# The start address of one operand: the token sums of the second feed-forward part, from 128 to 64 modulo 256 bytes

## The reference

```python
def _swiglu(x, w_gate, w_up, w_down):
    return (jax.nn.silu(x @ w_gate) * (x @ w_up)) @ w_down

h = _layer_norm(ALPHA * h + 0.5 * _swiglu(h, ffn2_w_gate[l], ffn2_w_up[l], ffn2_w_down[l]),
                ln4_g[l], ln4_b[l])
```

## Time and profile before

| | us |
|---|---|
| median of 3 runs | 1694.38 |
| lowest, highest run | 1690.96, 1695.35 |
| profiled execution | 1696.59 |
| its span, first to last instruction | 1694.9 |
| PE busy in the span | 1674.2 (99%) |
| DVE busy | 1098.7 (65%) |
| ACT busy | 742.0 (44%) |
| frames of the second feed-forward part | about 805 to 1002 us of the span |

### The profile page before, as it was taken

How to read it: one execution, slowest core, us unless ns; L and a number is a source line. 1 busy time by engine, 2 the same in 40 slices (tenths; PEclk the granted TensorE clock), 3 DMA queues, 4 the chain that set the end, 5 groups by cost and what they waited for, 6 DMA issues and landing times.

```text
span 1694.9 us, 24997 instructions
## 1 busy us (share of the span) xinstructions
PE 1674.2 (99%) x9222; PEld 1414.9 (83%) x9222; DVE 1098.7 (65%) x1489; ACT 742.0 (44%) x1099; POOL 167.8 (10%) x158
## 2 busy tenths in 40 slices
PE   9999999999999999998999999999999999999999
PEld 8888888788887888877999998877778787788887
DVE  5333338987974693669788774457976969744442
ACT  5222222246454374535555563345555455733231
POOL 0000000102005621013000001022101020000000
PEclk9999999999999999999999999999999999999999
DMA  6332347743121344232323335323232222233331
GB/s 217 99 99 89 96 136 227 221 136 107 63 90 60 125 149 137 90 97 67 108 99 114 109 113 164 108 88 119 84 100 84 87 90 80 79 121 112 107 105 63
DMA packets 51482, 188.13 MB, mean 111 GB/s; under 512 B 5776, under 2 KB 6288, under 8 KB 50512
## 3 DMA queue, kind: packets, MB, share of 16 engines
q1 hardware_dynamic: 44640, 161.50, 30.1%
q10 hardware_dynamic: 5184, 16.00, 3.0%
q0 software_dynamic: 1584, 9.60, 1.6%
HBM read 182.89 MB, written 4.19 MB: 110 GB/s over the span
## 4 chain that ended last, share of the span: by engine, by line
PE 51%; DVE 1%; issue 0%; ACT 0%
PE proj L439 41%; PE aux L439 6%; PE aux L2312 1%; PE aux L2299 1%; PE aux L2289 1%; PE aux L2292 0%; PE aux L583 0%; DVE xraw L1376 0%; DVE xsum L1381 0%; DVE hm L721 0%; PE aux L2337 0%; PE proj L2332 0%; PE aux L2327 0%; DVE a_lo L727 0%; DVE w_lo L431 0%
## 5 line engine op out<-in xcount | busy, mean ns | idle before, releaser
L431 DVE TENSOR_TENSOR w_lo<-raw,w_hi 128x1024 fp32r<-128x1024 f32 x260 | 331.3, 1276 | 305.4 <-ACT w_hi L424 299.8
L439 PE MATMUL proj<-a_hi,w_hi 128*128 128x512 f32 (+1 forms) x1336 | 510.4, 382 | 3.4 <-DVE a_lo L926 1.8
L439 PE MATMUL proj<-a_hi,w_lo 128*128 128x512 f32 (+1 forms) x1336 | 501.0, 375 | 0.0
L439 PE MATMUL proj<-a_lo,w_hi 128*128 128x512 f32 (+1 forms) x1336 | 500.6, 375 | 0.0
L424 ACT ACTIVATE w_hi<-raw 128x1024 fp32r<-128x1024 f32 x257 | 270.0, 1053 | 223.1 <-PE proj L439 146.4
L439 PEld LDWEIGHTS proj<-a_hi,w_hi 128*128 128x128 f32 x1336 | 251.6, 188 | 55.1 <-issue 5.5
L439 PEld LDWEIGHTS proj<-a_lo,w_hi 128*128 128x128 f32 x1336 | 251.3, 188 | 46.0 <-issue 2.9
L439 PEld LDWEIGHTS proj<-a_hi,w_lo 128*128 128x128 f32 x1336 | 251.0, 188 | 45.6
L439 PE MATMUL proj<-hid_hi,w_hi 128*128 128x512 f32 (+1 forms) x374 | 142.9, 382 | 1.4 <-DVE w_lo L431 1.4
L439 PE MATMUL proj<-hid_hi,w_lo 128*128 128x512 f32 (+1 forms) x374 | 141.0, 377 | 0.0
L439 PE MATMUL proj<-hid_lo,w_hi 128*128 128x512 f32 (+1 forms) x374 | 141.0, 377 | 0.0
(11 more groups left out here) (419 smaller groups left out, 2720.6 us busy)
## 6 DMA issues: line engine op xcount, KB each, us to landing
raw<-stream SPq DMA_DIRECT2D x303, 512.0 KB, 3.6
ctxk<-ada_in ACTq DMA_DIRECT2D x12, 512.0 KB, 4.3
ctxv<-ada_in ACTq DMA_DIRECT2D x12, 512.0 KB, 4.3
out<-h ACTq DMA_DIRECT2D x7, 256.0 KB, 2.0
h<-x_in SPq DMA_DIRECT2D x3, 512.0 KB, 8.6
btab<-rpb_in POOLq DMA_DIRECT2D x4, 384.0 KB, 3.5
cond_row<-cond_in ACTq DMA_DIRECT2D x1, 1024.0 KB, 6.2
side<-mem_in POOLq DMA_DIRECT2D x1, 1024.0 KB, 5.1
```

The costliest lines, as they stand in the source:

```text
L431: nc.vector.tensor_tensor(w_lo[:, st.slot], raw[:, st.slot], w_hi[:, st.slot].bitcast(F32), ALU.subtract).then_inc(lo_ready, 1)
L439: mm = nc.tensor.matmul(dst, a, b, start=start and n == 0, stop=stop and n == 2, skip_group_check=seeded)
```

## The change

One allocation of 48 float32 (192 bytes) per partition is put ahead of `xsum`. The `xsum` tensor starts at byte 193856 in place of 193664: at 64 modulo 256, as `ctx_hi` and `ctx_lo` do, in place of 128. Nothing is allocated after it in its phase, so no other tensor moves. The instructions of every engine, their order, their shapes and their waits are the same as before; the address of one operand differs in 960 matmuls, four ACT copies and four DVE subtractions.

```diff
             corner = sb("corner", [P, 2, HT], F32, ph)
             tsum = sb("tsum", [P, 3, T], F32, ph)
+            sb("under_xsum", [P, 48], F32, ph)
             xsum = sb("xsum", [P, 4, 2, 4, HT], F32R, ph)
```

## The result

| | before | changed |
|---|---|---|
| median, us | 1693.13 | 1696.03 |
| lowest, highest | 1688.76, 1697.4 | 1694.31, 1699.1 |
| runs | 22 | 22 |

The ratio is 1.0019, with a 95% interval of 1.0013 to 1.0026. I had forecast 1690.3 us, 4.1 us faster; it came out 2.9 us slower, by less than the 0.3% that I had set as the bound of "no change", but clear of noise over 22 runs. The spread says something too: the kernel before covers 8.6 us, the changed one 4.8.

A forecast was written before the change was run, and what follows sets the result against it. The prediction took PE's own matmul rate as the bound. Its terms, -4.3 us on the xsum matmuls and +0.16 us at the down projection, summed to -4.1 us: 1690.3 us from the median of 1694.4, range 1686.3 to 1695.8.

The forecast's parts named there:

- s = 113.3 ns: Frames, 960 matmuls moving xsum: step falls from 117.8 ns to the context rows' 113.3, saving 4.3 us.
- The 117.8 ns of the frames: Step per matmul in the frames before the change, read from two starts 16 frames apart, 158.30 us.
- its 2.2 us: Profiled execution's excess over the runs' median of 1694.4 us; the forecast was counted from the median.
- The rival of the distance: Frames: operand starts alike modulo 128 give xsum matmuls 120.0 ns, 2.1 us slower, 1696.5 us; chance 0.11.
- The 720 plain matmuls: Frames, matmuls moving the plain tokens: both addresses kept, so no change; neighbour effects costed at nothing.
- Who must keep up: Helpers in the frames: paced by PE; tightest handover, the corner sum, 1.64 us early, margin shrinking by 0.05 us.
- My own forecast frame: Changed kernel's frames: 16 should take 154.9 us in place of 158.3.
- the rival of the adding savings: Frames: savings of both starts add, xsum step 111.1 ns, 6.4 us saved less 0.24, 1688.2 us; chance 0.25.
- The writes of xsum: Eight instructions writing xsum before the frames: under 0.1 us by the destination's start, costed at nothing.
- The wait at the down projection: First matmul after the frames waits for DVE's weight split: 1.03 in place of 0.87 us, losing 0.16 us.
- 16-byte rule: SBUF has 16-byte cachelines and stepping between them costs; every start here is alike, so the change gives 0 us.
- independent read ports: Separate array ports for moving and stationary operands: stationary start should not matter, so 113.3 ns holds, 4.3 us saved.

The follow-up runs named there:

- after_again: The changed kernel, nothing edited, traced in a second execution: 1696.55 us.
- before_again: The kernel before the change, nothing edited, traced in a second execution: 1691.51 us.
- pairs: Computation left out: only 256-column matmuls, 96 for each of 16 pairs of moving and stationary starts, run twice in opposite orders; steps 113.3 to 120.0 ns.
- before_third: The kernel before the change, nothing edited, traced in a third execution: 1692.24 us.
- reset_x4: The kernel before with one of four sums, X4, moved 64 bytes further, its quarter at distance 0: median 1691.58 us, ratio 0.9985.

## Why the prediction was wrong

- *"I take s = 113.3 ns: it is the one row with this moving start, and the change is an alteration of the moving start."* This step failed. The rows held two addresses each, and I let one of them explain the difference. The quantity is their distance; the change took the sums from 64 to 128, where the step is 118.7 ns, and 118.8 was measured in the frames, in place of 113.3. The term was put at -4.3 us. Against the slow pattern that I had profiled it is 960 x (118.8 - 117.8) = +1.0 us, against the fast one 960 x 5.5 = +5.3.
- *The 117.8 ns of the frames* I took for the property of the kernel before. It was one of two patterns, and this execution stayed in it throughout. Two more showed 154.3 and 154.5 us for 16 frames, not 158.3. The sign that I passed over stood in the times: three runs spread over 4.4 us, and the profiled one was above all of them. I subtracted its 2.2 us as a constant; the slow pattern has a part in them, how large a part the timed runs don't show.
- *The rival of the distance* had the mechanism and the sign: +2.1 us forecast, +2.9 measured. I had given it 0.11. That the two numbers are near is luck: it counted from 117.8 ns, left the plain matmuls alone and had 120.0 ns for the sums (I reckoned modulo 128) against 118.7. I argued it down with "frames and context rows have the same distance, ... and yet 117.8 and 113.3 ns; so the distance can't be all". Equal distances with unequal steps should have led to the thought that the step has two values.
- *The 720 plain matmuls "keep both addresses: no change"*: wrong. They went from 117.8 to 115.5 ns on the mean, though their own distance stayed 64: the three plain quarters of a frame have 115.4, 117.8 and 113.3 ns, the same in every frame behind the first of both executions. What lies around them matters, and the quarter directly ahead is not all of it, since that is a sum quarter for each of the three. They gave back 720 x 2.3 = 1.7 us against the slow pattern, which is why the two profiled executions look alike: +1.0 - 1.7 us gives the 0.5 to 0.7 us that the frames gained there. Against the fast pattern they lost 720 x 2.2 = 1.6 us. My term was nothing, with a reason (six changes of kind in a frame) that took the effect to reach one matmul; it reaches whole quarters.
- *Who must keep up*: right for the changed kernel, whose 9.86 us frames the helpers keep up with, wrong as a statement on 113.3 ns frames. I let the margin shrink by 0.05 us once; it shrinks by the difference of two periods in every frame, 9.60 - 9.52 = 0.08 us, and with the 0.6 us that went at once in the fourth frame 1.25 us were gone in a dozen frames. My own forecast frame, 154.9 / 16 = 9.68 us, would have stayed above the helpers' 9.60; the rival of the adding savings, 153.2 / 16 = 9.58, would have met that bound.
- *The writes of xsum* cost nothing, as said. The wait at the down projection was 1.01 us in the first trace, near the 1.03 forecast, but 0.88 in after_again, hardly more than before's 0.87; since the sum quarters did not get faster, the 1.01 does not bear the forecast out.
- The Trainium skill's 16-byte rule (SBUF — State Buffer, "Door 1: The DMA port swizzle") gave 0 us. The runs do not agree with it as a rule for matmuls: starts that are all multiples of 16 give 113.3 to 120.0 ns. The Trainium skill's independent read ports (TensorE: Matmul & The Clock Gate, "Step-by-step: what each phase is for") are not borne out in the same table, where nothing but the place of one operand relative to the other moves the step by 6.7 ns.

How the 2.9 us come about is then, I take it, a mean over executions. In both traces of the changed kernel 16 frames take 157.76 us; in the three of before they take 154.3 to 158.3. Over all 20 frames the changed kernel (after_again) loses 3.8 us to before_again and gains 0.6 on the execution of the earlier trace rows (195.00 us). A median difference of 2.9 lies between the two. Which pattern each of the 22 timed runs was in was not traced. The pattern is also not all that spreads the runs: the lower clock at the head of the frames cost nothing in one trace, 1.3 us in another and 2.6 in the third, and ahead of it, at 788 us, the three traces of before already lie up to 1.8 us apart.

## What to carry to other kernels

A step read from one execution may be one of several that the same code can have: look first at how far the timed runs spread and where the profiled one lies among them, and profile a second and a third execution before a fraction of a per cent is argued. Of two operands' addresses ask for their distance before either start, and measure the pairs by themselves: one small kernel with all 16 pairs would have shown 118.7 ns where this forecast put 113.3. A gain in rate on the busiest engine ends where its helpers' own round begins, and a margin is used up by the difference of the two periods in every turn, not once.

## What the runs showed of the hardware that I had not expected

- Back-to-back 128 x 256 matmuls, each with its own weight load, at a granted clock of 1.00: the step depends on the stationary start less the moving start modulo 256 bytes, 120.0, 118.7 and 117.8 ns at 0, 128 and 192, and 113.3 or 117.8 at 64 (pairs).
- At distance 64 there are two steady patterns, and a stretch of 96 matmuls kept the one into which it fell (pairs). A wait of a tenth of a microsecond or so was followed by the slower one in three traces (before_again, before_third, reset_x4), and by a return to the faster one several times (122.3 ns at 917 us in before_again).
- With 512 columns distance 0 is among the best (226.7 ns) and 64 among the worst (233.3; the slowest, 96, had 234.2).
- The durations hardly tell: the median for xsum stayed at 281 ns while the step went from 117.8 to 118.8. Only the starts show it.
- After PE's wait of 3.6 to 3.7 us ahead of the frames the granted clock went to 0.50 in eight of nine traced executions of whole kernels, with steps of 213 ns, and stayed at 1.00 in the ninth (before_again). Where it fell the loss was about 1.3 to 2.6 us.
